# First chunks of a stage reordered by weight quarter, and four moves of small work in a two-block transformer kernel

## The chip, the cores and the metric

One Trainium2 chip, one core. The metric is the device time of one execution in microseconds (us), as the median of several executions. In the profile PE is TensorE, DVE is VectorE, ACT is ScalarE, POOL is GpSimd and SP is SyncE, whose queue issues the transfers.

## The reference

256 rows of width 1024, float32 throughout. Two layers of a first block, then one layer of a second:

```python
for l in range(DEPTH):                       # 2
    proj = h @ w_in[l]                       # to 1536 columns: q, k, v of two attentions
    ...                                      # rotary + global attention; windowed attention with sinks
    mix = jnp.concatenate([oa, ob], axis=-1) @ w_o[l]
    h = layer_norm(DEEPNORM_ALPHA * h + mix, ln1_g[l], ln1_b[l])
    ffn = peer_ffn(h, peer_wq[l], peer_keys[l], peer_u[l], peer_v[l])   # 16384 experts
    h = layer_norm(DEEPNORM_ALPHA * h + ffn, ln2_g[l], ln2_b[l])

u = rmsnorm(h, norm_mix_pre)                 # second block
proj = u @ w_in                              # conv part, then q, k, v and gates
...                                          # short convolution; compressed, selected, window attention
h = h + rmsnorm(mixed @ w_out, norm_mix_post)
mn = rmsnorm(mem, norm_mem)                  # memory rows, with keys and values mn @ w_kv_x
...                                          # cross attention with w_q_x, w_o_x
h = h + rmsnorm((jax.nn.silu(g) * up) @ w_down, norm_ffn_post)
```

## The kernel before, in words

**Split products.** Each float32 product is made of three: weights and activations are split into a rounded high part and the rest (the low part), and high x high, high x low and low x high are summed in PSUM. `xh` and `xl` hold the transposed activations (8 blocks of 128 by 256 rows), `wh` and `wl` the parts of one weight chunk.

**Chunks and quarters.** Weights stream from HBM in chunks of 1 MB (256 columns of all 1024 rows) into a `ring` of two slots; SP issues chunk c + 2 when both lows' engines have released the slot (`chunk_free`). A chunk is worked in four quarters (two row blocks each). For quarter q ScalarE rounds the high part as soon as TensorE has released the quarter of the chunk before (`high`, L1100, waits `parts_free[q]`); GpSimd subtracts the low part of quarters 0 to 2 (`low`, L471), VectorE that of quarter 3 (`low`, L1580); then `parts_ready[q]` lets TensorE run 12 matmuls of it, 48 for a chunk (`rows_by_chunk` L705, `chunk_by_cols` L722). Chunks alternate between PSUM slots 0 and 1, but in peer_wq all use slot 0. Quarter 3 is released by whoever empties the PSUM slot (`take_rows`, `evac`).

**The first chunk of a stage** (`first_rows` L639, `first_cols` L663) runs when `xh` has only just been made and `xl` not yet: ScalarE copies the transposes from PSUM to `xh` (`to_xT`, L1150), VectorE subtracts `xl` (`low_xT`, L1602) and releases PSUM slots 2 and 3 (`slot_free[2 + t]`). Before, all 32 matmuls with `xh` come first (L651, L675), then the 16 with `xl` (L657, L682), and only those release the quarters. `first_rows` serves w_in and w_o in both layers and w_o_x; `first_cols` serves peer_wq in both layers, the conv chunks of w_in_2, w_q_x and gate_up.

**w_in of the first block.** Chunks 0 to 3 hold the windowed attention's columns. VectorE copies each result out (`take_proj`, L1674). Behind chunk 3 it scales the two memory row tiles (L1705, after a reciprocal root that GpSimd makes), squares part of the projection (L1711, L1712), and then makes the low part of chunk 4. TensorE transposes the memory rows (L625) between chunks 4 and 5. After chunk 5 the keys and values of the memory (w_kv_x) are made in quarters beside the attention.

**End of the attention.** Per unit, VectorE asks GpSimd for a reciprocal root (`power`, L463; the value `rstd = ve ** -0.5`) and scales the output (L1786), which TensorE then transposes for w_o. The last of these roots stands in GpSimd's program behind low parts 0 and 1 of w_o's chunk 0.

**Between the stages.** The 16 MB `arena` holds the experts' gates during the expert stage, and everything else at other times. VectorE hands it over with `arena_free`; SP waits for that ahead of the memory rows (layers) and ahead of the gain row and nine constants (block 2). The gain row of block 2 also waits for `gain_free[1]`, which the layer norm's end gives. In block 2 VectorE makes the angles of the rotary tables (L2034 to L2051), ScalarE their sines (L1374, L1375), and VectorE the tables (L2057, L2058), all between chunk 0 and chunk 1 of the conv chunks.

The order of each engine's work is the order of the program text; the queues wait only by semaphores.

Of the kernel before, what the change touches and what calls it, by code (L numbers as in the profile page):

```python
# [8 lines left out]
P = 128  # L9
# [32 lines left out]
def build(nc, A, out):  # L42
# [4 lines left out]
    with ctx:  # L47
# [152 lines left out]
        dve_lows_done = sem("dve_lows_done")  # L200
        x_in = sem("x_in")
# [82 lines left out]
        def _(sp):  # L284
# [115 lines left out]
            gain(1, A["norm_mix_pre_2"], block2=True)  # L400
# [38 lines left out]
        def _(pool):  # L439
# [57 lines left out]
            for l in range(DEPTH):  # L497
# [66 lines left out]
                low(0, 0)  # L564
                low(0, 1)
                power(4, 28)
# [46 lines left out]
        def _(pe):  # L613
# [25 lines left out]
            def first_rows(full):  # L639
# [3 lines left out]
                for t in range(TT):  # L643
                    xh_in(t)
                    for q in range(4):
                        if t == 0:
                            pe.wait_ge(parts_ready[q], 1)
                            pe.sem_inc(parts_ready[q], -1)
                        for k in range(2):
                            for i, w in enumerate((wh, wl)):  # L650
                                pe.matmul(PS[:, t, 0:CW], xh[:, 2 * q + k, t * P:(t + 1) * P],  # L651
                                          w[:, q, k * CW:(k + 1) * CW], start=q + k + i == 0, stop=False)
                for t in range(TT):
                    pe.wait_ge(slot_free[2 + t], 1)
                    for q in range(4):
# [3 lines left out]
                        if t and q < 3:  # L659
                            last.then_inc(parts_free[q], 1)  # L660
                last.then_inc(full[0], 1)

            def first_cols(full):  # L663
# [3 lines left out]
                for t in range(TT):  # L667
                    xh_in(t)
                for q in range(4):
                    pe.wait_ge(parts_ready[q], 1)  # L670
                    pe.sem_inc(parts_ready[q], -1)
                    for b in range(2):
                        for k in range(2):
                            for i, w in enumerate((wh, wl)):
                                pe.matmul(PS[:, b, 0:S], w[:, q, k * CW + b * P:k * CW + (b + 1) * P],  # L675
                                          xh[:, 2 * q + k, :], start=q + k + i == 0, stop=False)
                for t in range(TT):
                    pe.wait_ge(slot_free[2 + t], 1)
                for q in range(4):
                    for b in range(2):  # L680
                        for k in range(2):
                            last = pe.matmul(PS[:, b, 0:S], wh[:, q, k * CW + b * P:k * CW + (b + 1) * P],  # L682
                                             xl[:, 2 * q + k, :], start=False, stop=q + k == 4)
# [408 lines left out]
        def _(act):  # L1092
# [9 lines left out]
            def high_parts(n, between=None, result=None, peel=0, late=None, following=False):  # L1102
# [16 lines left out]
                if peel:  # L1119
# [1257 lines left out]
```

## Time and profile before

| what | value |
|---|---|
| median of 3 runs | 2707.2 us (2700.27 to 2709.19) |
| profiled execution, its own time | 2714.95 us |
| its span | 2711.9 us |
| mean granted TensorE clock | 0.938 |
| busy: TensorE, VectorE, ScalarE, GpSimd | 91%, 63%, 49%, 26% |
| one low part on VectorE (L1580), mean of 961 | 0.708 us |

The profile is of one execution; its own time is 7.75 us above the median. Busy shares are of the span. A matmul whose end is modelled counts somewhat longer than its slot, so idle times in the rows are shorter than from slot to slot. An idle time in brackets stands before the row's instruction, with the line of the wait that ended it; a wait for several semaphores is one entry.

### The profile page before, as it was taken

What the parts mean: (1) busy time and instruction counts of PE and PEld (TensorE: products, weight loads), DVE (VectorE), ACT (ScalarE), POOL (GpSimd) and SP (SyncE); (2) the same over time, 40 slices, a digit from 0 to 9 for tenths busy, and PEclk for the clock granted to TensorE, in tenths of its full rate; (3) what the DMA queues carried; (4) which work ended last, traced back from release to release, by engine and by line L of the source; (5) the groups of instructions that cost most, each with busy time, mean ns of one, the idle gap of its engine ahead of it and who ended that gap; (6) DMA issues with size and microseconds to landing.
All of it is one profiled execution on the core that took longest, in us unless ns stands there. A gap on an engine that the chain in (4) does not pass through costs nothing. (4 is left out here: it accounts for less than half of the span.)

```text
span 2711.9 us, 56543 instructions
## 1 busy us (share of the span) xinstructions
PE 2479.2 (91%) x16295; PEld 2274.7 (84%) x16295; DVE 1717.9 (63%) x3804; ACT 1336.4 (49%) x2348; POOL 699.0 (26%) x532
## 2 busy tenths in 40 slices
PE   6879999999999998878999999999997978777998
PEld 6869999999888887778999999888886956666996
DVE  4646777887777775645777787777777244424126
ACT  3434555676555554434555676555554412222443
POOL 4545544000000002555445000000000500322655
PEclk9889999999999999889999999999998985677999
DMA  6234666444566665333566444566665431112543
GB/s 221 71 117 148 216 229 228 155 159 174 204 240 241 242 239 198 120 121 124 196 230 219 174 158 174 185 238 245 236 247 206 144 132 62 70 71 86 172 177 139
DMA packets 97756, 475.17 MB, mean 175 GB/s; under 512 B 11777, under 2 KB 13313, under 8 KB 50433
## 3 DMA queue, kind: packets, MB, share of 16 engines
q1 hardware_dynamic: 97104, 472.91, 49.2%
q10 hardware_dynamic: 560, 1.19, 0.1%
q8 instruction: 40, 0.66, 0.1%
q14 instruction: 52, 0.42, 0.0%
HBM read 438.41 MB, written 35.65 MB: 175 GB/s over the span
## 5 line engine op out<-in xcount | busy, mean ns | idle before, releaser
L1100 ACT ACTIVATE wh<-ring 128x512 fp32r<-128x512 f32 x1428 | 884.6, 627 | 644.7 <-ACTq L1099 641.8
L1580 DVE TENSOR_TENSOR wl<-ring,wh 128x512 fp32r<-128x512 f32 x961 | 674.8, 708 | 282.5 <-DVEq L1579 265.3
L471 POOL TENSOR_TENSOR wl<-ring,wh 128x512 fp32r<-128x512 f32 x295 | 386.2, 1328 | 1491.9 <-POOLq L470 1486.9
L910 PE MATMUL PS<-xh,wh 128*128 128x256 f32 x2048 | 594.3, 290 | 4.1 <-PEq L906 2.6
L910 PE MATMUL PS<-xl,wh 128*128 128x256 f32 x2048 | 581.0, 284 | 0.0
L910 PE MATMUL PS<-xh,wl 128*128 128x256 f32 x2048 | 580.8, 284 | 0.0
L745 PE MATMUL PS<-wh,xh 128*128 128x512 f32 x1112 | 435.6, 392 | 7.0 <-PEq L742 6.8
L745 PE MATMUL PS<-wl,xh 128*128 128x512 f32 x1112 | 433.7, 390 | 0.0
L745 PE MATMUL PS<-wh,xl 128*128 128x512 f32 x1112 | 433.7, 390 | 0.0
L910 PEld LDWEIGHTS PS<-xh,wh 128*128 128x128 f32 x2048 | 394.4, 193 | 8.7 <-issue 8.6
L910 PEld LDWEIGHTS PS<-xl,wh 128*128 128x128 f32 x2048 | 394.7, 193 | 0.0
L910 PEld LDWEIGHTS PS<-xh,wl 128*128 128x128 f32 x2048 | 394.0, 192 | 0.0
L580 POOL TENSOR_TENSOR wl<-ring,wh 128x512 fp32r<-128x512 f32 x144 | 208.6, 1449 | 226.8 <-POOLq L579 226.6
L745 PEld LDWEIGHTS PS<-wh,xh 128*128 128x128 f32 x1112 | 209.4, 188 | 54.6 <-issue 11.3
L745 PEld LDWEIGHTS PS<-wh,xl 128*128 128x128 f32 x1112 | 209.4, 188 | 44.0
L745 PEld LDWEIGHTS PS<-wl,xh 128*128 128x128 f32 x1112 | 209.4, 188 | 43.5 <-issue 0.5
L722 PE MATMUL PS<-xh,wh 128*128 128x256 f32 x688 | 197.2, 287 | 10.5 <-PEq L718 10.5
L722 PE MATMUL PS<-xl,wh 128*128 128x256 f32 x688 | 195.8, 285 | 0.0
L722 PE MATMUL PS<-xh,wl 128*128 128x256 f32 x688 | 195.7, 284 | 0.0
L1281 ACT ACTIVATE stg<-PS 128x256 f32<-128x256 f32 x256 | 97.8, 382 | 158.0 <-ACTq L1276 94.4
L1347 ACT ACTIVATE xh<-gains 128x256 fp32r<-128x256 f32 x248 | 103.5, 417 | 133.8 <-ACTq L1345 133.0
L625 PE MATMUL PS<-ident,arena 128*128 128x128 f32 (+1 forms) x407 | 75.8, 351 | 97.9 <-PEq L622 97.1
(276 smaller groups left out, 3807.2 us busy)
## 6 DMA issues: line engine op xcount, KB each, us to landing
ring<-in_peer_u SPq DMA_DIRECT2D x128, 1024.0 KB, 4.7
ring<-in_peer_v SPq DMA_DIRECT2D x128, 1024.0 KB, 4.8
acts<-stg SPq DMA_DIRECT2D x124, 256.0 KB, 2.1
gains<-acts SPq DMA_DIRECT2D x124, 256.0 KB, 4.8
ring<-in_w_in SPq DMA_DIRECT2D x24, 1024.0 KB, 4.8
ring<-in_w_gate_up SPq DMA_DIRECT2D x22, 1024.0 KB, 4.8
ring<-in_peer_wq SPq DMA_DIRECT2D x16, 1024.0 KB, 4.8
ring<-in_w_down SPq DMA_DIRECT2D x11, 1024.0 KB, 4.7
```

What stands on the lines that cost most here:

```text
L471: part = pool.tensor_tensor(wl[:, q, :], ring[:, s, q * QW:(q + 1) * QW], wh[:, q, :].bitcast(F32), SUB)
L580: pool.tensor_tensor(wl[:, q, :], ring[:, s, q * QW:(q + 1) * QW], wh[:, q, :].bitcast(F32), SUB).then_inc(parts_ready[q] if q == 0 else p ...
L625: last = pe.transpose(dst, src, ident[0:n, 0:n])
L722: last = pe.matmul(PS[:, 2 * s + b, 0:S], w[:, q, k * CW + b * P:k * CW + (b + 1) * P], x[:, 2 * q + k, :], start=q + k + i == 0, stop=q + ...
L745: last = pe.matmul(acc[:, t, c * 512:(c + 1) * 512], wst[x][:, j, t * P:(t + 1) * P], w[:, q, :], start=begin and j + i == 0, stop=end and ...
L910: last = pe.matmul(PS[:, 2 * j, 0:S], w[:, q, k * P:(k + 1) * P], x[:, at, :], start=at + i == 0, stop=at + i == 9)
L1100: act.activation(wh[:, q, :], ring[:, s, q * QW:(q + 1) * QW], ACT.Copy).then_inc(high_ready[q], 1)
L1281: last = act.activation(stg[:, s, j * S:(j + 1) * S], PS[:, 2 * j, 0:S], ACT.Gelu)
L1347: act.activation(wst[0][:, j, :], buf[:, j * S:(j + 1) * S], ACT.Copy).then_inc(cast_ready[j], 1)
L1580: part = dve.tensor_tensor(wl[:, q, :], ring[:, s, q * QW:(q + 1) * QW], wh[:, q, :].bitcast(F32), SUB)
```

## The change

1. In `first_rows` and `first_cols` the remainders (the matmuls with `xl`) run quarter by quarter, behind the first two quarters of the second tile or of the columns, and each quarter is released when its own remainders are done.
2. In `take_proj`, the low part of chunk 4 stands ahead of the scaling of the memory rows, that of chunk 5 ahead of the squares.
3. GpSimd's last root of an attention stands ahead of low part 1.
4. The arena is handed over ahead of the last expert pair's weights; block 2's gain row has a semaphore of its own and no longer waits for the layer norm.
5. VectorE's angles stand behind low parts of conv chunks 1 and 2, the tables behind the last conv chunk; ScalarE's sines stand behind the highs of chunk 4.

```diff
@@ sync @@
-            gain(1, A["norm_mix_pre_2"], block2=True)
+            sp.dma_start(gains2[:, 0, :], A["norm_mix_pre_2"].partition_broadcast(P)).then_inc(mixgain_in, 16)
@@ gpsimd @@
                 power(4, 20)
                 low(0, 0)
+                power(4, 28)
                 low(0, 1)
-                power(4, 28)
                 low(0, 2)
@@ tensor, first_rows @@
+                def high(t, q):
+                    for k in range(2):
+                        for i, w in enumerate((wh, wl)):
+                            pe.matmul(PS[:, t, 0:CW], xh[:, 2 * q + k, t * P:(t + 1) * P],
+                                      w[:, q, k * CW:(k + 1) * CW], start=q + k + i == 0, stop=False)
+                xh_in(0)
+                for q in range(4):
+                    pe.wait_ge(parts_ready[q], 1)
+                    pe.sem_inc(parts_ready[q], -1)
+                    high(0, q)
+                xh_in(1)
+                for q in range(2):
+                    high(1, q)
                 for t in range(TT):
                     pe.wait_ge(slot_free[2 + t], 1)
-                    for q in range(4):
+                for q in range(4):
+                    if q > 1:
+                        high(1, q)
+                    for t in range(TT):
                         for k in range(2):
                             last = pe.matmul(PS[:, t, 0:CW], xl[:, 2 * q + k, t * P:(t + 1) * P],
                                              wh[:, q, k * CW:(k + 1) * CW], start=False, stop=q + k == 4)
-                        if t and q < 3:
-                            last.then_inc(parts_free[q], 1)
+                    if q < 3:
+                        last.then_inc(parts_free[q], 1)
@@ tensor, first_cols: high(q) is all of quarter q with xh @@
+                for q in range(2):
+                    high(q)
                 for t in range(TT):
                     pe.wait_ge(slot_free[2 + t], 1)
                 for q in range(4):
+                    if q > 1:
+                        high(q)
                     for b in range(2):
@@ scalar @@
-            high_parts(N_CONV + N_PROJ2 - 2, to_xT_and_trig)
+            high_parts(N_CONV + N_PROJ2 - 2, squares_to_xT, peel=2, mid=trig)
@@ vector @@
-                dve.sem_inc(arena_free, 1)
+                if l == 0:
+                    dve.sem_inc(arena_free, 1)
...
-                    if c:
+                    if 0 < c < 4:
                         low(c % 2, 3)
...
                 take_proj(3)
+                low(0, 3)
                 if l == 0:
                     dve.wait_ge(memrstd_ready, 1)
...
                 take_proj(4)
-                own(dve.engine_nop())
+                low(1, 3)
                 qk_squares(256, 512)
...
+                own(dve.engine_nop())
+                dve.sem_inc(arena_free, 1)
                 weights(1, back[1])
...
+            beside = {1: reduced_angles, 2: angles}
+            for c in range(N_CONV):
+                if c:
+                    low(c % 2, 3)
+                if c in beside:
+                    beside[c]()
+                take_conv(c % 2, slice(2 * c, 2 * c + 2))
+            tables()
```

How the program's order moves is seen at three places. Names are those of the program's buffers, in the form written<-read, with the semaphores waited for in brackets.

TensorE in `first_rows`, w_in of layer 0: before, from the last matmul with `xh`, `wl` to chunk 1 (the sixteen `xl` matmuls stand together):

```order
L651 MATMUL PS<-wl,xh 128x256
L657 MATMUL PS<-wh,xl 128x256 [waits slot_free2]
L657 MATMUL PS<-wh,xl 128x256 x7
L657 MATMUL PS<-wh,xl 128x256 [waits slot_free3]
L657 MATMUL PS<-wh,xl 128x256 x7
L705 MATMUL PS<-wh,xh 128x256 [waits slot_free1,parts_ready0]
```

And now, from the end of the 24th matmul on:

```order
L648 MATMUL PS<-wl,xh 128x256
L666 MATMUL PS<-wh,xl 128x256 [waits slot_free3,slot_free2]
L666 MATMUL PS<-wh,xl 128x256 x7
L648 MATMUL PS<-wh,xh 128x256
...
L666 MATMUL PS<-wh,xl 128x256 x4
L648 MATMUL PS<-wh,xh 128x256
...
L666 MATMUL PS<-wh,xl 128x256 x4
L723 MATMUL PS<-wh,xh 128x256 [waits slot_free1,parts_ready0]
```

Eight remainder matmuls (quarters 0 and 1) have moved ahead of the second tile's last eight matmuls, and the waits for both halves of `xl` with them.

VectorE in w_in of layer 0, from the copy of chunk 3's result to that of chunk 4's, before:

```order
L1674 COPY arena<-PS 128x2x256 [waits dve_own,dve_full1]
L1705 SCALAR_TENSOR_TENSOR arena<-arena,rstdm 128x1024 [waits memrstd_ready,memgain_in]
L1705 SCALAR_TENSOR_TENSOR arena<-arena,rstdm 128x1024
L1715 ISA
L1711 TENSOR_TENSOR arena<-arena 128x2x256 [waits dve_own]
L1712 TENSOR_REDUCE ve<-arena 128x2x4 [waits dve_own]
L1580 TENSOR_TENSOR wl<-ring,wh 128x512 [waits dve_own,high_ready3]
L1674 COPY arena<-PS 128x2x256 [waits dve_own,dve_full0]
```

And now (the low part is the `wl<-ring,wh` row):

```order
L1697 COPY arena<-PS 128x2x256 [waits dve_own,dve_full1]
L1602 TENSOR_TENSOR wl<-ring,wh 128x512 [waits high_ready3]
L1729 SCALAR_TENSOR_TENSOR arena<-arena,rstdm 128x1024 [waits dve_own,memrstd_ready,memgain_in]
L1729 SCALAR_TENSOR_TENSOR arena<-arena,rstdm 128x1024
L1739 ISA
L1735 TENSOR_TENSOR arena<-arena 128x2x256 [waits dve_own]
L1736 TENSOR_REDUCE ve<-arena 128x2x4 [waits dve_own]
L1697 COPY arena<-PS 128x2x256 [waits dve_own,dve_full0]
```

The low part has moved ahead of both scalings and the squares.

ScalarE at the conv chunks of block 2, from the second `xh` copy on, before:

```order
L1150 ACTIVATE xh<-PS 128x8x128 [waits act_full3]
L1374 ACT_TABLE_LOAD [waits ang_ready]
L1374 ACTIVATE arena<-arena 128x96
L1375 ACTIVATE arena<-arena 128x96
L1123 UNCONDITIONAL_BRANCH
L1100 ACTIVATE wh<-ring 128x512 [waits chunk_in1,parts_free0]
```

And now, with the sixteen highs of chunks 1 to 4 cut to their ends:

```order
L1171 ACTIVATE xh<-PS 128x8x128 [waits act_full3]
L1118 ACTIVATE wh<-ring 128x512 [waits chunk_in1,parts_free0]
...
L1118 ACTIVATE wh<-ring 128x512 [waits parts_free3]
L1394 ACT_TABLE_LOAD [waits ang_ready]
L1394 ACTIVATE arena<-arena 128x96
L1395 ACTIVATE arena<-arena 128x96
L1144 UNCONDITIONAL_BRANCH
L1118 ACTIVATE wh<-ring 128x512 [waits chunk_in1,parts_free0]
```

Chunks 1 to 4 no longer have the table load in front of them, chunk 5 has.

## Rows read from the trace of the kernel before

**Rows 1.** The waits of TensorE over the whole span: us in total, times, longest us.

```profile
PE PS L625 <- PEq L622: 137.0, 29, 16.4
```

**Rows 2.** Timeline, w_in chunks 0, 1, layer 0: start, duration, engine, line, [idle before <-releaser].

```profile
24.64 2.08 PE L657 MATMUL PS<-wh,xl 128*128 128x256 f32 x16
...
28.36 0.35 PE L705 MATMUL PS<-wh,xh 128*128 128x256 f32 x1 [1.64 <-PEq L701]
...
26.94 4.22 POOL L471 TENSOR_TENSOR wl<-ring,wh 128x512 fp32r<-128x512 f32 x3 [5.60 <-POOLq L470]
```

**Rows 3.** Timeline, TensorE: peer_wq chunks 1 and 2 in layer 0, gate_up chunk 1.

```profile
200.87 0.36 PE L722 MATMUL PS<-xh,wh 128*128 128x256 f32 x1 [1.14 <-PEq L718]
...
207.94 0.36 PE L722 MATMUL PS<-xh,wh 128*128 128x256 f32 x1 [0.20 <-PEq L718]
...
2508.22 0.36 PE L722 MATMUL PS<-xh,wh 128*128 128x256 f32 x1 [0.92 <-PEq L718]
```

**Rows 4.** Timeline, w_o_x chunk 1: TensorE, then VectorE.

```profile
2468.66 0.36 PE L705 MATMUL PS<-wh,xh 128*128 128x256 f32 x1 [1.12 <-PEq L701]
...
2462.92 1.46 DVE L1496 CUSTOM_DVE_ANT_0 arena<-arena 128x256 f32<-128x256 f32 x1 [0.28 <-DVEq L1440]
...
2466.59 1.77 DVE L1580 TENSOR_TENSOR wl<-ring,wh 128x512 fp32r<-128x512 f32 x1
```

**Rows 5.** Timeline, w_in chunk 4 and after: both layers; TensorE, VectorE, ScalarE.

```profile
56.73 0.55 PE L705 MATMUL PS<-wh,xh 128*128 128x256 f32 x1 [4.07 <-PEq L701]
...
59.63 3.33 PE L625 MATMUL PS<-ident,arena 128*128 128x128 f32 x15
...
1091.54 0.36 PE L705 MATMUL PS<-wh,xh 128*128 128x256 f32 x1 [3.10 <-PEq L701]
...
1093.06 1.91 PE L625 MATMUL PS<-ident,arena 128*128 128x128 f32 x16
...
48.12 3.56 DVE L1705 SCALAR_TENSOR_TENSOR arena<-arena,rstdm 128x1024 f32<-128x1024 f32 x2
...
54.63 1.80 DVE L1580 TENSOR_TENSOR wl<-ring,wh 128x512 fp32r<-128x512 f32 x1 [0.26 <-DVEq L1579]
...
1083.89 2.47 DVE L1705 SCALAR_TENSOR_TENSOR arena<-arena,rstdm 128x1024 f32<-128x1024 f32 x2
...
75.35 1.70 ACT L1177 ACTIVATE arena<-arena 128x256 f32<-128x256 f32 x4 [3.91 <-ACTq L1173]
```

**Rows 6.** Timeline, end of layer 0's attention: GpSimd, VectorE.

```profile
147.76 1.01 POOL L463 TENSOR_TENSOR rstd<-ve,mhalf 128x4 f32<-128x4 f32 x1 [0.20 <-POOLq L470]
...
146.59 0.99 DVE L1770 TENSOR_SCALAR ve<-ve 128x4 f32<-128x4 f32 x1 [0.15 <-DVEq L1440]
```

**Rows 7.** Timeline at block 2's start; then the windows view (PEclk third from last).

```profile
2094.86 1.23 DVE L1548 TENSOR_TENSOR arena<-h,arena 128x1024 f32<-128x1024 f32 x1 [1.51 <-DVEq L1509]
...
2111.85 0.55 PE L722 MATMUL PS<-xh,wh 128*128 128x256 f32 x1 [3.49 <-PEq L718]
...
2112.00:2115.00 3.00, 3.00 (x15) 3.00 (x16) 1.49 (x1) 0.12 (x1) 2.63 (x2) 0.50 0.00 0
```

**Rows 8.** Timeline, conv chunks 1 to 5: ScalarE, TensorE, VectorE.

```profile
2107.99 1.28 ACT L1374 ACT_TABLE_LOAD   x1 [5.91 <-ACTq L1373]
...
2109.64 2.17 ACT L1100 ACTIVATE wh<-ring 128x512 fp32r<-128x512 f32 x4
...
2134.38 1.15 ACT L1100 ACTIVATE wh<-ring 128x512 fp32r<-128x512 f32 x2 [1.59 <-ACTq L1099]
...
2137.47 0.28 PE L722 MATMUL PS<-xh,wh 128*128 128x256 f32 x1
...
2126.47 0.69 DVE L2063 COPY arena<-PS 128x512 f32 x1 [4.37 <-DVEq L1573]
```

**Rows 9.** Timeline, w_o_x chunk 0: second half of xl, and TensorE's matmul 25.

```profile
2456.83 1.23 DVE L1602 TENSOR_TENSOR xl<-PS,xh 128x1024 fp32r<-128x1024 f32 x1 [0.49 <-PEq L637]
...
2458.32 0.28 PE L651 MATMUL PS<-wh,xh 128*128 128x256 f32 x1
```

More of the change, by code:

```diff
@@ L200, in build @@
         dve_lows_done = sem("dve_lows_done")
+        mixgain_in = sem("mixgain_in")
         x_in = sem("x_in")
@@ L666, in first_cols, with cols, high @@
                 pe.sem_inc(slot_free[0], -1)
-                for t in range(TT):
-                    xh_in(t)
-                for q in range(4):
+                def cols(b, k):
+                    return slice(k * CW + b * P, k * CW + (b + 1) * P)
+                def high(q):
                     pe.wait_ge(parts_ready[q], 1)
@@ L1100, in high, with high_parts @@
                 act.activation(wh[:, q, :], ring[:, s, q * QW:(q + 1) * QW], ACT.Copy).then_inc(high_ready[q], 1)
-            def high_parts(n, between=None, result=None, peel=0, late=None, following=False):
+            def high_parts(n, between=None, result=None, peel=0, late=None, following=False,
+                           mid=None):
                 for q in range(4):
@@ L1117, in chunk @@
                         late(c - 2, s)
-                if peel:
-                    chunk(1, 1, False)
-                    chunk(2, 0)
+                for i in range(peel):
+                    chunk(2 * i + 1, 1, i > 0)
+                    chunk(2 * i + 2, 0)
+                if mid:
+                    mid()
                 if n > 2:
@@ L2052, in _, with reduced_angles @@
[L2052 to L2059 removed]
+            def reduced_angles():
+                for i in range(9):
+                    dve.wait_ge(consts_in[i], 16)
+                own(dve.tensor_copy(posv[:, :], pos_f[:, :].bitcast(I32)))
+                own(dve.tensor_tensor(a3[:, 0, :, :], bc(posv[:, :].unsqueeze(2), 3, 32),
+                                      bc(invf[:, :].unsqueeze(1), 3, 32), MUL))
+                magic = 1.5 * 2.0 ** 23
+                own(dve.tensor_scalar(angs[:, 1, :], angs[:, 0, :], 1 / (2 * math.pi), magic, MUL, ADD))
+                own(dve.tensor_scalar(angs[:, 1, :], angs[:, 1, :], magic, None, SUB))
+                c1 = 6.28125
+                c2 = round((2 * math.pi - c1) * 2 ** 20) / 2 ** 20
+                c3 = 2 * math.pi - c1 - c2
+                for at, (src, c) in enumerate(((0, c1), (2, c2), (3, c3))):
+                    own(dve.scalar_tensor_tensor(angs[:, 2 + at, :], angs[:, 1, :], -c, angs[:, src, :], MUL, ADD))
@@ L2061, in take_conv, with tables @@
+            def tables():
+                dve.wait_ge(trig_ready, 1)
+                dve.sem_inc(trig_ready, -1)
+                for half in range(2):
+                    c = slice(32 * half, 32 * half + 32)
+                    dve.tensor_copy(rope2[:, 0, :, c], a3[:, 7, :, :])
+                    dve.tensor_scalar(rope2[:, 1, :, c], a3[:, 6, :, :], 1.0 if half else -1.0, None, MUL)
+                own(dve.engine_nop())
             def take_conv(s, at):
```

82 lines of the change are left out of this document (24 added, 58 removed).

## The prediction

> **What bounds the kernel now.** I read the page first: TensorE is busy for 91% of the span (the table above). In nearly every stage the question is therefore whether TensorE waits, and only waits that it has can be taken out. The table of TensorE's waits comes next: it waits most, 137 us, at the borders of stages, for the rows that it is to transpose (L625) [rows 1]. Which waits the change can reach is read from the timelines, place by place. What a reader is to see there: a column of matmuls with 256 columns runs at a pitch of (2.08 - 0.28) / 15 = 0.12 us at the full clock, so a chunk of 48 takes 5.76 us; ahead of the second chunk TensorE stands still for 1.64 us [rows 2].
>
> **First chunk's remainders by quarter.** Before, quarter 0 of the weights is released only after matmul 42 of the 48 (`first_rows`), 6 x 0.12 = 0.72 us ahead of the end. The last matmul's slot ends at 24.64 + 16 x 0.12 = 26.56 and TensorE starts again at 28.36, 1.80 us later (1.64 by the view, which counts the last matmul 0.16 us longer) [rows 2]. So rounding (ScalarE), subtracting (GpSimd) and seeing it takes 0.72 + 1.80 = 2.52 us. After the change quarter 0 is released after matmul 28, that is 20 x 0.12 = 2.40 us ahead of the end: 0.12 us of wait are left. Quarters 1 and 2 follow at GpSimd's 4.22 / 3 = 1.4 us each [rows 2], and TensorE uses a quarter in 12 x 0.12 = 1.44 us; quarter 3 is VectorE's. That is tight, so I take 1.5 us at each of four places (w_in and w_o in both layers, the same 1.64 at each): 4 x 1.5 = 6.0 us, bounds 0 and 6.7.
> In `first_cols` the release moves from matmul 36 to 20 of 48, that is 3.36 us ahead of the end against a need of 1.44 + 1.08 = 2.52 us, the same as above. In gate_up the wait was 0.92 us [rows 3] (1.08 with the 0.16), in w_q_x as long: 2 x 1.0 = 2.0 us. In peer_wq it was 1.14 us (1.30) [rows 3], but there the second chunk uses the same PSUM slot and waits until ScalarE has emptied it. Later chunks, whose releases are early, have the same wait behind the key scores: the chunk begun at 200.87 has its last slot end 5.82 us later, at 206.69, and the next begins at 207.94, 1.25 us later [rows 3]. So 0.05 each comes back: 0.1 us.
> For w_o_x, VectorE decides. After the first 1.64 us TensorE waits 1.12 us more, for quarter 3, since VectorE first squares and scales the first chunk's result. Those squares took 1.46 us while GpSimd subtracted, and the low part 1.77 us [rows 4], against a mean of 0.71 us for all such low parts (the table above). If VectorE stays as late, the gain here is nothing; if GpSimd's earlier work leaves it alone, up to 1.64. I take 1.0.
>
> **Low parts ahead of memory scaling.** In layer 0 VectorE does 3.56 us of scaling and the squares ahead of the low part of chunk 4's last quarter, which then begins at 54.63 and takes 1.80 us; TensorE stands for 4.07 us until 56.73 and comes back at the half clock [rows 5]. Its last 12 matmuls last from 56.73 to the first transpose at 59.42 (one ahead of 59.63), 2.69 us; in layer 1, at the full clock, from 1091.54 to 1093.06, 1.52. The 16 transposes last until 62.96, 3.54 us, against 1.91 in layer 1 [rows 5]. Put where the scaling began, at 48.12, the low part is done by 49.9 even if it takes 1.80, and TensorE wants quarter 3 at 56.73 - 4.07 = 52.66. Gain: 4.07 + 1.17 + 1.63, about 6.85 us. Layer 1: 3.10 + 0.08, about 3.2 us, its clock having stayed up. Next to be late would be the scaled memory rows: 49.9 plus 3.56 us for both scalings is 53.5, against 52.5 + 1.44 = 53.9 where TensorE now comes to the transposes. It just fits. For chunk 5 VectorE waits for ScalarE in front of the squares (under 1 us), while TensorE still has 36 matmuls, 4.3 us, to do. On SP the kv chunk that follows has the 2 MB of bias ahead of it in either kernel; ScalarE rounds it ahead of the first exponentials, in front of which it stood idle for 3.91 us [rows 5], so its lateness is covered up to that; past it, each us would cost one per layer. Together 10.05 us.
>
> **Reciprocal root ahead of one low part.** In layer 0 GpSimd begins the root at 147.76, behind two low parts; VectorE's request, stretched to 0.99 us beside them, had begun at 146.59 [rows 6]. With one low part (1.4 us) less in front, the root follows a request that is not stretched: about 1.2 us, bounds 0 and 1.4. In layer 1 the root was not held up, only VectorE's work ahead of it was slowed: 0.5, same bounds. Together 1.7 us. What GpSimd holds back now is low part 1, which TensorE wants only after the transposes and the first quarter.
>
> **Block 2.** The gain row no longer waits for the layer norm. VectorE stood 1.51 us for it at 2094.86 [rows 7]; it is now asked for before the norm begins: 1.5 us. The nine constants ride along. In front of conv chunk 1 TensorE stood 3.49 us, since ScalarE had first to wait for the angles and load the sine table (2107.99), then round quarter 0 [rows 7, 8]. Afterwards it ran at a granted 0.50 [rows 7]: from 2111.85 to 2137.47, where chunk 5 starts [rows 8], are 25.62 us for 192 matmuls, 23.04 at full pitch, so 2.58 more. With quarter 0 released early and the table load gone from there, 3.49 + 2.5 = 6.0 us come back. The sines now stand in front of chunk 5's rounding, which began at 2134.38 after an idle of 1.59 us. Load and sines take 1.28 us and, until rounding begins at 2109.64, 0.37 more [rows 8], 1.65 in all, so they push it by 0.1. Rounding and subtracting take some 2.1 us, and TensorE starts chunk 5 at 2137.47, 3.09 us after 2134.38 [rows 8]: nothing. VectorE's angles are less than the 5.91 us for which ScalarE stood idle for them [rows 8]; they now lie in two conv chunks and the tables, shorter, in a third, in each of which VectorE idles for 4.37 us [rows 8]: nothing. If that cover went, each us late would be paid once.
> The Trainium skill, *ScalarE: Activation LUTs*, "What ACT_TABLE_LOAD costs", counts about 2.66 us for a change of table, a drain included. By it ScalarE would be held for about 1.4 us more, TensorE for 0.5, and the sum would be 27.9; no row here shows the drain, since the engine had been idle before.
> The early hand-over of the arena between the layers moves 1.5 MB of memory rows and gain forward, behind both ring chunks that were issued before. In layer 1 VectorE scales those rows at 1083.89 with no idle ahead [rows 5], so nothing was waiting for them: nothing.
>
> **Sum.** 6.0 + 2.0 + 0.1 + 1.0 + 10.05 + 1.7 + 1.5 + 6.0 = 28.4 us. Against the profiled execution: 2714.95 - 28.4 = 2686.6. That execution stands 7.75 us above the median of the three runs, 2707.2; the same sum from the median gives **2679 us** (2678.8).
>
> **Rivals.** (1) *The wait moves from quarter 0 to quarter 3 of the second chunk.* w_o_x shows it: 1.12 us for VectorE's part [rows 4]. VectorE's low part cannot begin before ScalarE has seen the first chunk's result taken. If this happened at all places, 6.0 + 2.0 + 1.0 would be lost: 2707.2 - 19.4 = 2687.8. For it: 1.80 us for a low part beside GpSimd. Against: after the other first chunks VectorE has only a copy to do, and quarter 3 is wanted 4.3 us after the end. Chance 0.15.
> (2) *The scaling becomes late.* Both scalings collide with GpSimd's next low parts and TensorE waits at the memory transposes, at the half clock again: about half of the 6.85 and 3.2 us is given back: 2707.2 - 23.4 = 2683.8. The margin of 0.4 us speaks for it; against it, that both bounds used are the slow ones. Chance 0.12.
> (3) *The gains do not add up or are not passed on*, since the kv chunks, GpSimd's rotation or a transfer set the time after chunk 5: under 8 us are left, 2701. GpSimd takes two low parts before the root that starts the rotation, and they can wait for the ring. Chance 0.05.
> (4) *Slower: the second half of xl.* TensorE now waits for both halves after 24 matmuls (rows) or 16 (columns) where it waited after 32 and 40 (rows) or 32 (columns). At w_o_x the second half is ready at 2456.83 + 1.23 = 2458.06, and matmul 25 ran at 2458.32 [rows 9]: 0.26 us of margin. Were the halves later by more than 28.4 / 10 = 2.8 us at each of the ten places, all would be lost; a wait like that of 3.49 us also brought the half clock, 2.5 us: 10 x (3.49 + 2.5) - 28.4 = 32 slower, 2739. Against: nothing moves the subtractions later, and the margin is positive even here. Chance 0.03.
>
> **How the numbers follow.** The forecast has 0.65. Its own bounds are w_o_x and the roots (about 3 us), the 1.64s, and the spread of the runs, 2700 to 2709. The range goes from 2672 to 2693 and takes in rivals 1 and 2. Within 0.3%, 8 us, is what measurements cannot tell from no change. Faster by more: forecast, rivals 1 and 2, 0.92; same: rival 3, 0.05; slower 0.03.
>
> **What would show it.** Right: the idle of 1.64 and 0.92 us ahead of second chunks under 0.3; no 4.07, 3.10 and 3.49 us; a granted clock of 1.00 through the conv chunks; no idle on VectorE ahead of the gain multiply; the peer_wq wait still 1.1 us. Wrong: idle at the fourth quarter of second chunks beyond w_o_x, a wait in front of the memory transposes or the first remainder matmuls, or the same stalls with other releasers.

## The result, and the profile after

The changed kernel took 2675.1 us (median of 4 runs, 2672.9 to 2677.5) against 2708.2 us for the kernel before in the same series: ratio 0.989, 95% interval 0.986 to 0.991, 33.1 us less. One of the four runs before took 2837.9 us; without it the median before is the 2707.2 us of the table above, and the difference 32.1 us. Forecast were 28.4 us less and 2679 us. Two later series of the same kernel gave 2674.9 and 2674.4 us.

| | before | after |
|---|---|---|
| profiled execution, its own time | 2714.95 us | 2672.89 us |
| span | 2711.9 us | 2670.2 us |
| mean granted TensorE clock | 0.938 | 0.950 |
| one low part on VectorE, mean of 961 | 0.708 us | 0.717 us |

The two profiled executions are 41.7 us apart in span, 8.6 us more than the medians; experiment 5 shows about 10 us of the 41.7 that come and go between executions. Their pages, first lines of section 1, before and after:

```profile
PE 2479.2 (91%) x16295; PEld 2274.7 (84%) x16295; DVE 1717.9 (63%) x3804; ACT 1336.4 (49%) x2348; POOL 699.0 (26%) x532
PE 2451.2 (92%) x16295; PEld 2252.1 (84%) x16295; DVE 1728.8 (65%) x3804; ACT 1338.7 (50%) x2348; POOL 694.8 (26%) x532
```

The same 16295 matmuls kept TensorE busy for 28.0 us less, and it was idle for 13.7 us less. So two thirds of the 41.7 us are matmuls that ran at a higher granted clock, and one third is wait.

TensorE's waits (us in total, times, longest), two rows of before and three of after, to be read beside [rows 1]:

```profile
PE PS L705 <- PEq L701: 22.8, 15, 4.1
PE PS L722 <- PEq L718: 10.5, 17, 3.5
...
PE PS L626 <- PEq L623: 142.5, 33, 16.3
PE PS L723 <- PEq L719: 7.8, 6, 2.6
PE PS L740 <- PEq L736: 5.5, 16, 1.1
```

The transposes wait (L626) for 5.5 us more than before. `rows_by_chunk` (L723 now) waits for 7.8 us in 6 places where it had 22.8 in 15 as L705; `chunk_by_cols` (L740) for 5.5 where it had 10.5. Those two are 20.0 us less; with the 5.5 us given back at the transposes that leaves 14.5, about the 13.7 us above.

The timeline of the changed kernel, w_in of layer 0: TensorE (chunk 1, chunk 3's quarter 3, the memory transposes), GpSimd behind the first chunk, VectorE at chunk 4. It answers to [rows 2] and [rows 5].

```profile
28.05 0.36 PE L723 MATMUL PS<-wh,xh 128*128 128x256 f32 x1
...
45.60 0.35 PE L723 MATMUL PS<-wh,xh 128*128 128x256 f32 x1 [1.48 <-PEq L719]
...
53.95 1.91 PE L626 MATMUL PS<-ident,arena 128*128 128x128 f32 x16
...
26.61 3.80 POOL L472 TENSOR_TENSOR wl<-ring,wh 128x512 fp32r<-128x512 f32 x3 [3.90 <-POOLq L471]
...
48.31 1.84 DVE L1602 TENSOR_TENSOR wl<-ring,wh 128x512 fp32r<-128x512 f32 x1
50.71 3.52 DVE L1729 SCALAR_TENSOR_TENSOR arena<-arena,rstdm 128x1024 f32<-128x1024 f32 x2 [0.56 <-DVEq L1727]
```

Chunk 1 begins with no idle in front, since GpSimd begins at 26.61 instead of after the whole chunk. Chunk 4's low part begins at 48.31, takes 1.84 us as expected beside GpSimd, and the 4.07 us are gone. The 16 memory transposes take 1.91 us, as in layer 1, with no wait: the scaled rows are in time. One wait is longer: 1.48 us ahead of chunk 3's quarter 3 where the kernel before had 0.97. It is not the change's: the two later traces of the same kernel have 0.97.

First column chunks and w_o_x, after: peer_wq chunk 1 of layer 0, then w_o_x chunk 1 at quarter 3, and what VectorE did before it. They answer to [rows 3] and [rows 4].

```profile
192.37 0.36 PE L740 MATMUL PS<-xh,wh 128*128 128x256 f32 x1 [1.08 <-PEq L736]
...
2428.93 0.36 PE L723 MATMUL PS<-wh,xh 128*128 128x256 f32 x1 [2.29 <-PEq L719]
...
2423.32 1.40 DVE L1517 CUSTOM_DVE_ANT_0 arena<-arena 128x256 f32<-128x256 f32 x1 [0.28 <-DVEq L1460]
...
2425.23 1.73 DVE L1550 TENSOR_TENSOR arena<-arena,gains 128x512 f32<-128x512 f32 x1 [0.15 <-DVEq L1460]
2426.88 1.75 DVE L1602 TENSOR_TENSOR wl<-ring,wh 128x512 fp32r<-128x512 f32 x1
```

peer_wq still waits, 1.08 for 1.14 us. At w_o_x the wait of 1.64 us ahead of chunk 1 is gone and the one at its quarter 3 has grown from 1.12 to 2.29 us. Over all traces described below it is 2.29 or 2.30 in the five with the early start of chunk 1 and VectorE's old order, and 1.12 or nothing in the six without the early start.

Block 2, after: GpSimd's last root in layer 0 and TensorE behind it (to [rows 6]); TensorE in front of block 2's transposes; ScalarE's table load (to [rows 7] and [rows 8]); TensorE at quarter 3 of conv chunks 2 and 3; then two of VectorE's angle operations.

```profile
141.01 1.01 POOL L464 TENSOR_TENSOR rstd<-ve,mhalf 128x4 f32<-128x4 f32 x1 [0.79 <-POOLq L471]
...
143.82 1.94 PE L626 MATMUL PS<-ident,arena 128*128 128x128 f32 x8 [4.62 <-PEq L623]
...
2083.66 3.65 PE L626 MATMUL PS<-ident,arena 128*128 128x128 f32 x16 [15.02 <-PEq L623]
...
2114.72 0.63 ACT L1118 ACTIVATE wh<-ring 128x512 fp32r<-128x512 f32 x1 [1.52 <-ACTq L1117]
2115.37 1.28 ACT L1394 ACT_TABLE_LOAD   x1
2116.67 0.28 ACT L1394 ACTIVATE arena<-arena 128x96 f32<-128x96 f32 x1
...
2106.35 0.36 PE L740 MATMUL PS<-xh,wh 128*128 128x256 f32 x1 [0.28 <-PEq L736]
...
2112.77 0.36 PE L740 MATMUL PS<-xh,wh 128*128 128x256 f32 x1 [0.43 <-PEq L736]
...
2099.83 1.39 DVE L2062 TENSOR_TENSOR arena<-arena 128x96 f32<-128x96 f32 x1
...
2102.76 0.21 DVE L2066 TENSOR_SCALAR arena<-arena 128x96 f32<-128x96 f32 x1 [0.16 <-DVEq L1460]
```

No wait is left in front of conv chunk 1, where 3.49 us had been. The wait ahead of block 2's transposes was 16.42 us and is 15.02. The table load sits where it was meant to, and TensorE does not wait behind it (in one of the other traces it waits there for 0.55 us). VectorE's angles do cost something: 0.28 and 0.43 us at the fourth quarters behind them. The operation of 1.39 us ran while GpSimd subtracted (2098.38 to 2102.55), the one of 0.21 us just after.

Of what the prediction named as signs of being right, the 1.64, 0.92, 4.07, 3.10 and 3.49 us are gone, the granted clock from conv chunk 1 to the end of chunk 5 is 1.00, and peer_wq waits for 1.08 us. Of the signs of being wrong one is there in small: the waits at fourth quarters, 0.28 and 0.43 us.

**How the stages are compared below.** One profiled execution of a kernel is not enough: the same stage without any edit in it differs by a few us between executions. For every experiment the start of each stage on TensorE was read from the timeline, and each stage's length put against that of the kernel before. With 14 executions, those that have an edit stand against those that have not. "Like for like" means this: mean of those without less mean of those with. Left out are executions with another edit in the same place (experiment 4 for w_in, experiments 4 and 6 for w_o_x). "The cross attention" is counted from w_q_x's chunk 1 to the transposes for w_o_x, block 2's attention from its first product to the transposes for w_out.

### The profile page after: what moved, and what is told of

Read it like the earlier page. It is cut to its first block and busy times, and to the rows that moved or that the text cites. A ratio compares the mean times of both kernels' runs of the same rounds, so it can differ in the third digit from the quotient of the medians.

```text
span 2670.2 us, 56531 instructions
## 1 busy us (share of the span) xinstructions
PE 2451.2 (92%) x16295; PEld 2252.1 (84%) x16295; DVE 1728.8 (65%) x3804; ACT 1338.7 (50%) x2348; POOL 694.8 (26%) x532
## 5 line engine op out<-in xcount | busy, mean ns | idle before, releaser
L1602 DVE TENSOR_TENSOR wl<-ring,wh 128x512 fp32r<-128x512 f32 x961 | 684.2, 717 | 276.8 <-DVEq L1601 260.3
L740 PE MATMUL PS<-xh,wh 128*128 128x256 f32 x688 | 195.9, 285 | 5.5 <-PEq L736 5.5
L740 PE MATMUL PS<-xl,wh 128*128 128x256 f32 x688 | 194.6, 283 | 0.0
L740 PE MATMUL PS<-xh,wl 128*128 128x256 f32 x688 | 194.6, 283 | 0.0
L626 PE MATMUL PS<-ident,arena 128*128 128x128 f32 (+1 forms) x407 | 71.8, 338 | 102.3 <-PEq L623 101.6
```

What stands on the lines that cost most here:

```text
L626: last = pe.transpose(dst, src, ident[0:n, 0:n])
L740: last = pe.matmul(PS[:, 2 * s + b, 0:S], w[:, q, k * CW + b * P:k * CW + (b + 1) * P], x[:, 2 * q + k, :], start=q + k + i == 0, stop=q + ...
L1602: part = dve.tensor_tensor(wl[:, q, :], ring[:, s, q * QW:(q + 1) * QW], wh[:, q, :].bitcast(F32), SUB)
```

## Experiments

All ratios are against runs of the kernel before on the same chip in the same series (medians 2708.65, 2708.5 and 2707.0 us).

**1. Only the first chunks reordered.** The kernel before with the two TensorE hunks of the change.

```diff
+                for q in range(2):
+                    high(1, q)
...
+                    if q < 3:
+                        last.then_inc(parts_free[q], 1)
```

> Only the first chunks are reordered; all else is the kernel before. The stages of the changed kernel's trace gave, place by place, w_in 1.7 and 2.4, w_o 1.1 and 1.4, w_q_x 2.5, gate_up 1.3, peer_wq about 0, w_o_x about 0 us. Theory (the removed waits are passed on and add): about 10 us less than the kernel before, 8 to 12, with conv chunk 1 still waiting over 3 us for the angles and the sine table. Rival (granted clock): about 15 us of the 33 came in block 2's attention and the cross attention with no edit there; if the reordering itself keeps the clock up, this kernel gains over 15 and shows those stretches at the changed kernel's times (78.6 us for the attention where before had 88.7). Rival (waits move to quarter 3): under 5 us.

Measured: 2688.7 us (2687.5 to 2690.9), ratio 0.9929 (0.9912 to 0.9946): 20 us less by the medians, twice the theory's 10. The cross attention took 4.8 us less; block 2's attention stayed at 88 us. Conv chunk 1 still waits, for 2.00 us, and the stretch from block 2's transposes to it is as long (14.56 us) as in experiments 2, 7 (alone) and 9, none of which has the block 2 edits. By stages, like for like, the reordering gives 15.3 us (the table below), so some 5 of its 20 us are not traced. Its trace also has 0.86 us instead of 3.10 ahead of chunk 4's quarter 3 in layer 1, with VectorE's squares at 0.69 us instead of 1.82 and its low part at 0.69 instead of 1.81. No other trace with the old order there has that, so it is not put down to the edit.

**2. Only the low parts of w_in moved.**

```diff
                 take_proj(3)
+                low(0, 3)
...
                 take_proj(4)
-                own(dve.engine_nop())
+                low(1, 3)
```

> Only the low parts of chunks 4 and 5 of w_in stand ahead of the memory scaling and squares, in both layers. Theory: 6.85 + 3.2 = 10.05 us less, by the changed kernel's trace 7.1 + 3.5 = 10.6, all of it between the start of chunk 4 and the attention's scores; nothing elsewhere. Rival (it shifts the transfers or the attention behind it): under 7 us, the missing part found in the attention of the same layer. Block 2's attention should be at 88.7 us as before if its clock is a matter of what the change does in block 2, and anywhere between 78 and 89 if it is a matter of the single execution.

Measured: 2698.9 us, 9.75 less by the medians; the runs spread from 2673 to 2707, ratio 0.9945 (0.9918 to 0.9971). The theory holds at the place: the stretch from the transposes behind chunk 3 to the start of chunk 5 is 7.07 us shorter than before in this kernel and in all others with the edit but experiment 4, chunk 4 of layer 1 3.3 us. Part of it is given back between chunk 5 and the end of the attention, as the rival had it, though less: 2.2 us in layer 0 here.

**3. Only the moves of block 2** (arena, gain row, angles, sines, tables).

```diff
+            rms_shared(tmp1, 1, mixgain_in)
...
-            high_parts(N_CONV + N_PROJ2 - 2, to_xT_and_trig)
+            high_parts(N_CONV + N_PROJ2 - 2, squares_to_xT, peel=2, mid=trig)
```

> Only the arena handed over early, the gain row's own semaphore, and the angles, sines and tables moved. Conv chunk 1 keeps the late release of quarter 0. Theory: gain row 1.5; conv chunk 1 waits about 1.6 us instead of 3.49 (the release alone), so 1.9 there, and up to 2.5 of half clock: 3.4 to 6 us less. Rival (clock): the wait of 3.49 us ahead of conv chunk 1 is what leads to the low clock in block 2's attention; then this kernel alone shows the attention at about 78 us and gains 13 to 16. Rival (arena): the early hand-over costs the last experts' weights time; then the end of each expert stage is longer than before by over 1 us.

Measured: 2703.95 us, 4.7 less by the medians, ratio 0.9985 (0.9968 to 1.0002), an interval that just takes in no change. The trace has 15.05 us ahead of block 2's transposes, 0.93 us ahead of conv chunk 1 (not 1.6: as at the other column chunks), and block 2's attention at 88.7 us. The clock rival, with its 13 to 16 us, falls. The arena rival is not supported: the experts' stage of layer 0 was as long as before here.

**4. Two more low parts moved.** The changed kernel, with VectorE's low part ahead of the squares in the residual stages, and ahead of the memory's squares for w_in's chunk 3.

```diff
@@ residual_rows @@
-                    if c:
-                        low(s, 3)
                     take_rows(s)
                     own(dve.tensor_copy(o_all[:, :, cols], PS[:, 2 * s:2 * s + 2, 0:CW]))
                     dve.sem_inc(slot_free[s], 1)
+                    if c < 3:
+                        low(1 - s, 3)
@@ w_in, behind chunk 2 @@
-                own(dve.engine_nop())
+                low(1, 3)
```

> The changed kernel with two more moves of VectorE's low part of quarter 3: in the residual stages (w_o_x, w_out and down) ahead of the squares of the chunk before, and in w_in for chunk 3 ahead of the memory rows' squares. Theory (VectorE's order decides the waits at quarter 3 that are left): the 2.29 us ahead of quarter 3 of w_o_x's chunk 1 and the 1.48 us ahead of that of w_in's chunk 3 go, with smaller ones in w_out and down: 3 to 6 us less than the changed kernel, 36 to 39 less than the kernel before. Rival (the squares are late instead and the norm's end waits for them): no gain over the changed kernel, the time coming back behind the last chunk of the residual stages.

Measured: 2676.5 us, ratio 0.9878 (0.9861 to 0.9895), no better than the changed kernel. The timeline of TensorE in w_in of layer 0 shows what became of the second move:

```profile
46.31 0.36 PE L723 MATMUL PS<-wh,xh 128*128 128x256 f32 x1 [0.76 <-PEq L719]
...
50.35 0.36 PE L723 MATMUL PS<-wh,xh 128*128 128x256 f32 x1 [0.69 <-PEq L719]
```

Chunk 3 has no wait left, but chunk 4 now has two, 0.76 us at its start and 0.69 us at its quarter 2: the wait was passed on. From chunk 1 to chunk 5 this kernel takes 28.01 us where the others with change 2 take 27.05 to 27.56, so the second move loses something. (Its target of 1.48 us was 0.97 in most executions.) The first move did what it should in w_out and w_o_x, and is tested alone in experiment 6.

**5. The changed kernel again,** twice.

> The changed kernel once more, to see what of its trace comes again. In its first trace block 2's attention took 78.6 us at a granted clock of 0.72 to 0.76 where the four other kernels and the one before had 88 to 89 at 0.50, and the experts of layer 0 took 4.7 us longer. Theory (chance of the single execution): the median comes again within 4 us of 2675, but this trace has the attention at 88 to 89 us and the experts of layer 0 elsewhere. Rival (the change does it): the attention is at 78 to 80 us again.

> The changed kernel a third time, beside the next one on the same chip. Block 2's attention took 78.6 us in one of its traces and 88.6 in the other. Theory (chance of the single execution): runs between 2662 and 2678, median near 2675, and the attention at one of the two times, nothing in between. Rival: a third time for the attention, which would make it a matter of degree.

Measured: 2674.9 us (2662.3 to 2675.8) and 2674.4 us (2669.5 to 2677.0). Block 2's attention took 88.7 us in both traces, against 78.6 in the first. The windows view of that attention, counted from its first transposes (PEclk third from last), in the first trace of the changed kernel and then in the second:

```profile
2242.20:2257.20 15.00, 14.99 (x51) 12.13 (x52) 4.09 (x8) 5.06 (x10) 0.00 (x0) 0.50 0.44 176
2257.20:2278.20 21.00, 19.58 (x96) 17.06 (x96) 12.13 (x22) 7.83 (x15) 0.00 (x0) 0.72 0.00 0
2278.20:2288.20 10.00, 7.43 (x56) 6.68 (x56) 6.59 (x14) 4.64 (x10) 0.00 (x0) 1.00 0.01 2
```

```profile
2238.80:2253.80 15.00, 14.97 (x50) 12.13 (x51) 4.07 (x8) 5.09 (x10) 0.00 (x0) 0.50 0.46 181
2253.80:2274.80 21.00, 21.00 (x81) 18.34 (x80) 9.98 (x17) 5.53 (x11) 0.00 (x0) 0.50 0.00 0
2274.80:2284.80 10.00, 10.00 (x39) 8.67 (x38) 3.81 (x7) 3.70 (x9) 0.00 (x0) 0.50 0.00 0
```

The same program on the same data: between 15 and 36 us in, one execution gets the full clock back, and then does 56 matmuls in 10 us where the other, busy without a pause at 0.50, does 39. So 10 us of the 41.7 between the two spans are a matter of the single execution. Of the 14 traces three show the higher clock here (the changed kernel's first, experiment 6's first and experiment 8), eleven the lower, and nothing in between beyond 0.9 us. All three stand among the eight traces of kernels that have changes 2 to 5 together, none among the other six. If the edits had no say, three would fall so in one case of about seven (56 of 364): that the changes make the higher clock more frequent is neither shown nor excluded.

**6. The low part ahead of the squares in the residual stages alone,** twice. The first half of experiment 4's diff.

> The changed kernel with one more move: in the residual stages (w_out, w_o_x, down) VectorE makes the low part of the next chunk's quarter 3 right behind the copy, ahead of the squares of the result. Theory (VectorE's order decides w_o_x): the 2.29 us ahead of quarter 3 of w_o_x's chunk 1 go; with w_out, where the kernel with both moves took 3.1 us less than the changed kernel, 4 to 6 us less than the changed kernel. Rival (the moves give nothing): that kernel's median was 2676.5, no better than 2675.1; then this one is within 2 us of the changed kernel too, and the trace must show where the 5 us were lost again.

> The changed kernel with the low part ahead of the squares in the residual stages, again. It was 12.6 us faster than the changed kernel by the medians of four runs each; its stages say 4 to 5 us (w_o_x 1.5, w_out 2 to 3.4), and its trace had the 78.6 us in block 2's attention. Theory (stages): 4 to 6 us faster than the changed kernel. Rival (the move also makes the higher clock in that attention more frequent): 10 to 14 us faster again.

Measured: 2662.3 us (2656.3 to 2667.8), ratio 0.9828 (0.9805 to 0.9851), then 2671.0 us (2661.0 to 2677.1), ratio 0.9861 (0.9836 to 0.9885): 12.6 and 3.4 us below the changed kernel of the same series. All nine runs have a median of 2663.1 us, against 2674.9 for all twelve of the changed kernel. The traces say 3.7 us: 1.65 in w_o_x and 2.07 in w_out (means of the three with this move against the three of the changed kernel and the second of experiment 7). VectorE behind w_o_x's first chunk in the first of the two:

```profile
2414.24 0.69 DVE L1540 COPY arena<-PS 128x512 f32<-128x512 f32 x1 [3.60 <-DVEq L1595]
2415.28 1.60 DVE L1602 TENSOR_TENSOR wl<-ring,wh 128x512 fp32r<-128x512 f32 x1 [0.35 <-DVEq L1601]
2417.26 1.33 DVE L1517 CUSTOM_DVE_ANT_0 arena<-arena 128x256 f32<-128x256 f32 x1 [0.37 <-DVEq L1460]
```

The low part ends 2.6 us after the copy began, where it took 6.3 us in the changed kernel (2422.35 to 2428.63), and TensorE has no wait within w_o_x any more. Part of that is not passed on: the wait ahead of the transposes behind it is 14.36 us instead of 11.90, since VectorE's last chunk sets it. This version is the fastest here. By how much beyond 3.7 us stays open. The time goes with the mean granted clock of the run: its five runs below 2664 us have 0.952 to 0.957, its four above 0.945 to 0.950, and of the changed kernel's twelve only the one at 2662.3 us has 0.955. That would fit with the higher clock of experiment 5 coming more often, but the second trace had that attention at 87.8 us, and the other runs have no trace that shows where they gained.

**7. The reordering in w_q_x alone, and everywhere but there.** `first_cols_x` is the function of the other kernel.

```diff
-            chunks(4, first_cols, chunk_by_cols, act_full)
+            chunks(4, first_cols_x, chunk_by_cols, act_full)
```

> The kernel before with the reordered first chunk in w_q_x alone. Its stall of 0.92 us was costed at 1.0. The three traces with the reordering have 4.6 to 6.2 us less in the cross attention behind it, with granted clocks of 0.84 there against 0.50 to 0.67, and the two without have not. Theory (the removed stall keeps the clock up for longer): 0.7 to 2.5 us less at the chunk and 4 to 5 in the cross attention, 5 to 7 in all, from this one edit. Rival (something ahead of w_q_x does it, such as the shorter stages before): about 1 us less, and the cross attention as before.

> The changed kernel with the old order of the first chunk in w_q_x alone. Theory: 5 to 7 us slower than the changed kernel, the stall of 0.92 us back, and the cross attention 4 to 5 us longer at a clock of 0.5 to 0.7. Rival: 1 us slower, the cross attention as in the changed kernel.

Measured: alone 2700.5 us, 8.0 less than the kernel before by the medians (ratio 0.9979, 0.9966 to 0.9992: 2 to 9 us); taken out of the changed kernel 2684.15 us, 9.2 more than the changed kernel of the same series. Windows of the first 14 us of w_q_x, the next 18 and the 38 that hold the cross attention's products: first with the edit alone, then the changed kernel without it; the last row is the 38 us of the kernel before.

```profile
2376.80:2390.80 14.00, 12.53 (x92) 12.34 (x93) 4.06 (x4) 5.67 (x9) 4.50 (x4) 0.89 0.11 46
2390.80:2408.80 18.00, 16.95 (x132) 16.47 (x131) 1.39 (x2) 5.91 (x10) 6.97 (x6) 1.00 0.58 206
2408.80:2446.80 38.00, 30.10 (x157) 26.62 (x156) 8.74 (x11) 9.30 (x16) 3.72 (x3) 0.82 0.08 28
```

```profile
2356.50:2370.50 14.00, 11.58 (x66) 11.07 (x67) 3.39 (x3) 4.51 (x7) 1.65 (x2) 0.68 0.11 48
2370.50:2388.50 18.00, 17.46 (x144) 17.11 (x143) 2.45 (x3) 6.57 (x12) 10.16 (x8) 1.00 0.56 197
2388.50:2426.50 38.00, 29.67 (x116) 25.20 (x117) 6.14 (x9) 7.51 (x15) 3.71 (x3) 0.73 0.01 5
```

```profile
2414.30:2452.30 38.00, 29.98 (x114) 25.09 (x115) 6.13 (x9) 7.26 (x14) 3.71 (x3) 0.68 0.01 3
```

One edit that takes 0.92 us of wait away is followed by a clock of 0.82 instead of 0.68 or 0.73 in a stretch 20 us later, in which nothing was edited. In all eight traces with it the cross attention is 4.8 to 6.5 us shorter than before, in the six without it within 0.35 us of before. That the edit brings this is shown, put in alone and taken out alone; why the clock answers so, no run shows.

**8. All but the first chunks.** The change without the hunks of experiment 1.

```diff
-                for q in range(2):
-                    high(1, q)
```

> All of the change but the reordered first chunks. Theory (parts add): the reordering was worth 20 us alone (2708.65 to 2688.7), so this one is about 20 us slower than the changed kernel, at 2695, with 1.64 us ahead of the second chunks of w_in, w_o and w_o_x, 0.92 at w_q_x and gate_up, and the cross attention at its old length. Rival (parts overlap, since the moved sines give nothing while quarter 0 is released late): 22 to 26 us slower, 2697 to 2701.

Measured: 2692.9 us (2688.9 to 2696.6), ratio 0.9955 (0.9940 to 0.9970): 18.5 more than the changed kernel of the same series, against 20 for the reordering alone. The parts add, within what can be measured: by the medians 20.0 (experiment 1), 9.75 (2) and 4.7 (3) less and 0.8 more (9) make 33.6, against 33.1 for all. Conv chunk 1 waits 0.92 us here, 2.00 with the reordering alone, nothing with both. This trace had the higher clock in block 2's attention, so that clock does not need the reordering.

**9. Only the root moved.**

```diff
                 low(0, 0)
+                power(4, 28)
                 low(0, 1)
-                power(4, 28)
```

> The last root of an attention ahead of low part 1, alone. It was costed at 1.2 us in layer 0 and 0.5 in layer 1. The stretch from the last transposes of layer 0's attention to chunk 1 of w_o is 2.0 us shorter in the changed kernel and 2.1 in the kernel with the reordering alone, so no gain of the root is seen there. Theory A (as costed): the wait ahead of the last transposes is 1.2 us shorter than 5.46 in layer 0. Theory B: the root begins earlier, but VectorE's request comes after low part 0 either way, so under 0.5 us; the median cannot show either, being within 3 us of the kernel before.

Measured: 2707.8 us, ratio 1.0012 (0.9994 to 1.0030): a gain of 1.7 us is just outside the interval, one of 1.2 inside it. TensorE at the two groups of the last transposes of layer 0's attention, here, and then in experiment 2, which has the old order:

```profile
147.11 1.06 PE L625 MATMUL PS<-ident,arena 128*128 128x128 f32 x8
153.48 1.94 PE L625 MATMUL PS<-ident,arena 128*128 128x128 f32 x8 [5.31 <-PEq L622]
```

```profile
141.46 1.94 PE L625 MATMUL PS<-ident,arena 128*128 128x128 f32 x8 [1.78 <-PEq L622]
...
147.57 1.94 PE L625 MATMUL PS<-ident,arena 128*128 128x128 f32 x8 [4.17 <-PEq L622]
```

The second wait alone misleads: it is 5.31 with the root moved and 4.17 us without, but the first group then has hardly a wait where it had 1.78. The two waits together are 5.2 to 5.8 us in the nine traces with the move and 5.9 to 6.4 in the five without, 0.6 less on the mean. In layer 1 they are 5.1 to 5.3 against 5.6 to 6.1, again 0.6. So the move gives 0.6 us in either layer: half of theory A in layer 0, a little more than theory B. The kernel before, from which the 1.2 us were read, has the longest of the five, 0.96 + 5.46.

## Why the prediction was right, and where its steps were not

The forecast (28.4 us less, 2679) was met in sign, range and size; measured were 33.1. By its own steps, with the gain like for like:

| term | forecast, us | measured, us |
|---|---|---|
| first row chunks, w_in and w_o, both layers | 6.0 | 1.94 + 1.33 + 1.55 + 1.78 = 6.60 |
| gate_up and w_q_x | 2.0 | 1.12 + 1.51 = 2.63 |
| cross attention behind w_q_x | not in the sum | 5.60 |
| peer_wq | 0.1 | 0.05, within the spread |
| w_o_x | 1.0 | 0.44, within the spread |
| low parts ahead of the scaling | 6.85 + 3.2 | to the end of the attention: 5.04 + 3.62 = 8.66 |
| root, by the length of the last transposes | 1.2 + 0.5 | 0.55 + 0.67 = 1.22 |
| gain row | 1.5 | 1.47 |
| conv chunks | 3.49 + 2.5 | to chunk 1 2.83, behind it 0.36 = 3.19 |
| sum | 28.4 | 29.9 |

Without the 5.6 us of the cross attention, the terms that the prediction did have come to 24.3 us of its 28.4. The 4.1 us that it had too much and the 5.6 that it left out nearly cancel, so that the total came this near is in part luck. The mechanisms were right but for the one left out.

The remaining 3.2 us to 33.1 are not traced to a stage. The experts' stages, 800 us each, differ between executions by up to 7 us (layer 0's: 2.5 shorter to 4.7 longer than before). Kernels with the block 2 edits have layer 0's 2.0 us longer on the mean, far less than that spread: whether the early hand-over costs something there stays open.

- **First chunks: right in mechanism.** GpSimd's start right behind quarter 0 and the price of a quarter were as reckoned. Of the "1.5 us at each of four places" the stretches gained 1.3 to 1.9. In every trace the waits of 1.64 and 0.92 us are gone wherever the reordering is in.
- **The term that failed by omission** is "w_q_x as long: 2 x 1.0". The prediction charged the half clock where it saw it directly behind a wait (conv, chunk 4), and at w_q_x it took the wait alone. The 5.6 us came in a stretch where nothing was edited (experiment 7).
- **Conv chunk 1: oversized.** The 6.0 us of "3.49 + 2.5" came back as 3.2, and both terms were those of one execution. The four other traces with the old order wait for 2.00 to 2.06 us instead of 3.49, though their stretch up to chunk 1 is as long, and behind it they are already 1.0 us shorter. From 2 us into conv chunk 1, the windows view of experiment 2 has a clock of 0.74 where [rows 7] has 0.50:

```profile
2112.00:2116.00 4.00, 4.00 (x28) 4.00 (x27) 0.00 (x0) 1.26 (x2) 2.51 (x3) 0.74 0.39 127
```

  In the changed kernel 0.28 + 0.43 us of this were spent again at VectorE's angles, costed at nothing since VectorE "idles for 4.37 us". Its operations took up to 1.39 us each beside GpSimd.
- **w_o_x: the lower bound was the right one.** VectorE stayed late, as the prediction's first case said ("the gain here is nothing"); its weight should have been on that, since nothing in the change touched the squares. The earlier start of chunk 1 went into the wait at quarter 3 (1.12 to 2.29 us). Experiment 6 shows the cause by removing it.
- **Low parts: right.** 7.07 and 3.3 us at the place, against 6.85 and 3.2. Like for like it is 6.2 in layer 0, since the trace of before was the worst of five there (the others have 1.2 to 1.4 us less, one 0.3), and 1.2 us of those are given back by the end of the attention; in layer 1 it is 3.7 with 0.1 given back. The scaling was in time, so rival 2 fell. Of rival 1 there is a little: a longer wait at quarter 3 in w_o_x and the two behind the angles. Rival 3 fell too, since most is passed on, and so did rival 4: no wait for xl shows.
- **Root: half.** The 1.2 us rested on one stretched request in one execution [rows 6]; the waits there are 0.6 us shorter, in layer 1 as well (experiment 9). This row of the table and the one above it adjoin, and their sum is surer than the split between them.
- **Table load.** The Trainium skill, *ScalarE: Activation LUTs*, "What ACT_TABLE_LOAD costs", has 2.66 us with a drain. Here ScalarE had rounded until 2115.35, loaded from 2115.37 for 1.28 us and began the sine at 2116.67. The trace agrees with the load and not with the drain: none shows, and the kept sum without it was the better one.

## What to carry to other kernels

Release shared operands in the order in which the next stage wants them, not after the last use of all; where the last engine in that chain has other work, its order decides, and that is the next thing to change. A short wait of TensorE can cost more in the clock of a later stretch than in itself, so cost it from the granted clock after it, in kernels with and without it. And before a term of 1 us is taken from one profiled execution, look whether the same stretch has the same length in a second one.

## What the runs showed of the hardware

- TensorE's granted clock takes one of two courses with identical work: in block 2's attention 0.50 for 46 us and more, or back to 1.00 within 36 us, 10 us apart in time (experiment 5; 3 of 14 traces the fast one). Single runs of one kernel reached from 2673 to 2707 us with mean clocks of 0.957 to 0.941 (experiment 2).
- Without the wait of 0.92 us at w_q_x the next stretch takes 49.6 to 51.3 us (8 traces), with it 55.8 to 56.5 (6 traces): 5.6 us for a wait of 0.92 (experiment 7).
- VectorE's low part took 0.69 us alone and up to 1.84 us while GpSimd subtracted; its angle operations on 96 elements, 0.21 to 0.26 us when alone, took up to 1.39 us there. Small work put "into idle time" is better costed at that rate.
- A change of ScalarE's table took 1.28 us between a rounding and a sine that stood back to back with it (2115.35 to 2116.67).
